# Squared-sum chain of the norm-carrying FFNs, and the block order of the first recurrent mixer

## The reference

```python
def swiglu(h, w1, w3, w2):
    return (jax.nn.silu(h @ w1) * (h @ w3)) @ w2

def half_ffn(x, g, w1, w3, w2):
    return x + FFN_RES * swiglu(rmsnorm(x, g), w1, w3, w2)

def mixer_gla_rglru(h, w_in, ...):               # second stack, layer 0
    q, k, v, g, lr, xr, xg = jnp.split(h @ w_in, MIX0_SPLITS, axis=-1)
    log_f = log_sigmoid(lr @ gla_gate_up + gla_gate_bias) / GLA_GATE_TEMP
    o = chunk_end_gated_linear_attention(q * GLA_DK ** -0.5, k, v, log_f)
    o = rmsnorm(o, gla_head_norm) * silu(g)
    y = rg_lru(causal_depthwise_conv(xr, conv_w, conv_b), lru_wa, lru_ba, lru_wx, lru_bx, lru_lambda)
    y = y * gelu(xg)
    return concatenate([o, y], axis=-1) @ w_out
```

## Time and profile before

| | |
|---|---|
| median of 3 runs | 2967.72 us (2962.85 to 2968.32) |
| the profiled execution | 2967.48 us, span 2965.7 us |
| mean granted TensorE clock | 0.964 of full |
| PE busy | 2743.1 us, 92% |
| POOL busy | 2202.6 us, 74% |
| ACT, DVE busy | 50%, 48% |

### The profile page before, as it was taken

How to read it: one execution, slowest core, us unless ns; L and a number is a source line. 1 busy time by engine, 2 the same in 40 slices (tenths; PEclk the granted TensorE clock), 3 DMA queues, 4 the chain that set the end, 5 groups by cost and what they waited for, 6 DMA issues and landing times.

```text
span 2965.7 us, 59967 instructions
## 1 busy us (share of the span) xinstructions
PE 2743.1 (92%) x21822; PEld 2640.5 (89%) x21822; DVE 1422.3 (48%) x2533; ACT 1483.4 (50%) x2242; POOL 2202.6 (74%) x1680
## 2 busy tenths in 40 slices
PE   8999999979999989999979989997799899998997
PEld 8989898868999989898868989987799799887997
DVE  2134525546556555435546554347533733645335
ACT  4444456445555554456435554455444544555445
POOL 8866666746978967575747968976799689766995
PEclk9999999999999999899989999999899999999999
DMA  6544433424554544343424544543455355433552
GB/s 240 184 149 161 135 131 126 163 86 135 184 170 157 184 156 150 118 151 121 164 93 135 184 149 157 184 149 114 143 185 184 124 180 184 151 130 131 186 184 86
DMA packets 123000, 452.12 MB, mean 152 GB/s; under 512 B 13650, under 2 KB 13650, under 8 KB 122196
## 3 DMA queue, kind: packets, MB, share of 16 engines
q1 hardware_dynamic: 121104, 441.43, 44.4%
q10 hardware_dynamic: 1732, 8.39, 0.8%
HBM read 448.72 MB, written 1.05 MB: 152 GB/s over the span
## 4 chain that ended last, share of the span: by engine, by line
POOL 52%; issue 29%; PE 15%; DVE 2%; ACT 1%; POOLq 1%; DVEq 0%; ACTq 0%
POOL wl L366 27%; POOL wl L367 25%; PE R L405 3%; PE R L401 3%; PE R L404 3%; PE Y L401 1%; PE Y L405 1%; PE Y L404 1%; PE R L549 1%; POOLq L372 0%; PE R L431 0%; PE R L434 0%; PE R L437 0%; DVE W L1920 0%; DVE XLB L1791 0%
## 5 line engine op out<-in xcount | busy, mean ns | idle before, releaser
L366 POOL TENSOR_TENSOR wl<-raw,wh 128x512 fp32r<-128x512 f32 x836 | 1107.8, 1325 | 743.2 <-ACT wh L1074 736.0
L401 PE MATMUL R<-XHB,wh 128*128 128x256 f32 (+1 forms) x4216 | 1205.7, 286 | 25.2 <-POOL wl L367 10.6
L405 PE MATMUL R<-XHB,wl 128*128 128x256 f32 (+1 forms) x4216 | 1198.1, 284 | 0.0
L404 PE MATMUL R<-XLB,wh 128*128 128x256 f32 (+1 forms) x4216 | 1193.9, 283 | 0.0
L367 POOL TENSOR_TENSOR wl<-raw,wh 128x512 fp32r<-128x512 f32 x836 | 1144.5, 1369 | 0.0
L1074 ACT ACTIVATE wh<-raw 128x1024 fp32r<-128x1024 f32 x836 | 878.4, 1058 | 348.2 <-PE R L401 237.0
L401 PEld LDWEIGHTS R<-XHB,wh 128*128 128x128 f32 x4216 | 804.2, 191 | 34.6 <-POOL wl L367 18.2
L404 PEld LDWEIGHTS R<-XLB,wh 128*128 128x128 f32 x4216 | 807.3, 191 | 1.4 <-issue 1.0
L405 PEld LDWEIGHTS R<-XHB,wl 128*128 128x128 f32 x4216 | 805.4, 191 | 0.0
L401 PE MATMUL Y<-BH,wh 128*128 128x256 f32 x1408 | 402.6, 286 | 20.9 <-DVE BL L1722 20.9
L404 PE MATMUL Y<-BL,wh 128*128 128x256 f32 x1408 | 401.1, 285 | 0.0
(11 more groups left out here) (400 smaller groups left out, 3260.0 us busy)
## 6 DMA issues: line engine op xcount, KB each, us to landing
raw<-in_stream SPq DMA_DIRECT2D x836, 512.0 KB, 3.3
G<-in_wcmp ACTq DMA_DIRECT2D x2, 2048.0 KB, 7.8
G<-in_mem ACTq DMA_DIRECT2D x2, 1024.0 KB, 5.9
TB<-in_table SPq DMA_DIRECT2D x1, 1312.0 KB, 13.1
X<-in_x SPq DMA_DIRECT2D x2, 512.0 KB, 5.8
out_dram<-X ACTq DMA_DIRECT2D x4, 256.0 KB, 2.2
WS<-in_mix_w ACTq DMA_DIRECT2D x2, 256.0 KB
G<-in_p ACTq DMA_DIRECT2D x2, 256.0 KB, 3.0
```

Source lines behind the costliest of these rows:

```text
L366: pool.tensor_tensor(wl[:, s, 0:512], raw[:, r, 0:512], wh[:, s, 0:512].bitcast(F32), ALU.subtract)
L401: i = pe.matmul(o, wh[w], hi, start=start, stop=False, skip_group_check=True)
L404: pe.matmul(o, wh[w], lo, start=False, stop=False, skip_group_check=True)
L405: i = pe.matmul(o, wl[w], hi, start=False, stop=stop, skip_group_check=True)
```

## The change

Three things are done.

1. In the seven FFNs DVE adds squares as the pieces are made: after the rests of piece 4, 6 and 7 it adds one pair of square chunks (512 columns) to W8[0:2]. The three adds of `late_root` go. PE sums the two chunks that are left with two matmuls right after `together`, into SQ, the upper half of the fourth Y bank. Three Y banks are zeroed only after the fourth block, ahead of the wait for the first hidden chunk, and the fourth behind that wait. No bank of R is held for the sum. In the ln kind the bank of the mean is handed back as soon as the last chunk is centred. S4 is made while ACT works on the first hidden chunk.
2. `gla` runs in another block order: xr, lr, k0, gate, k1, xg0 to xg3, LRU tiles, v, q0, key-values, q1, g0, state reads, g1, g2, sums, g3. The rows of the output projection are ordered LRU first, then heads.
3. In `gla` work moves from DVE to ACT: the first tap of the convolution, the gate's bias, the square inside gelu, the arguments and the square of the LRU's decay. DVE makes the LRU pieces first, and normalises each pair of heads apart.

PE, and ACT's part:

```diff
+        SQ = Y[:, 3, T:2 * T]
...
 
                 hi, lo, width = (XHB, XLB, T + 2) if kind == "ln" else (XH, XL, T)
-                for b in range(4):
-
+                def opened(b):
                     pe.matmul(Y[:, b, :], ZB[:, 0:P], ZB[:, :], start=True, stop=False, skip_group_check=True)
+
+                if kind == "first":
+                    for b in range(4):
+                        opened(b)
+                if kind == "ln":
+                    means(mean)
...
                     dense(hi, lo, width=width)
                     dense(hi, lo, width=width)
 
-                def down(f, end=None):
+                def down(f, end=None, opens=False):
+                    if opens:
+                        for b in range(3):
+                            opened(b)
                     from_dve()
+                    if opens:
+                        opened(3)
                     s = weights()
                     for c in range(DC):
                         three(Y[:, c // 2, (c % 2) * T:(c % 2) * T + T], (slice(None), s, slice(c * P, c * P + P)),
...
                 together(2, hi, lo, split_ready, width)
                 trips = (FC - 2) // 4
                 if kind != "first":
                     trips -= 1
+                    need(sq_added, 3)
+                    for c in range(2):
+                        i = pe.matmul(SQ, ONES, W8[:, c, :], start=c == 0, stop=c == 1, skip_group_check=True)
+                    i.then_inc(sum_ready, 1)
                     for j in range(4):
-                        dense(hi, lo, width=width)
-                        if j == 0:
-                            need(sq_summed)
-                            pe.matmul(sums[:, T:2 * T], ONES, W8[:, 0, :], start=True, stop=True,
-                                      skip_group_check=True).then_inc(chunk_ready, 1)
-                        dense(hi, lo, width=width)
-                        down(j)
+                        up_pair()
+                        down(j, opens=j == 0)
...
                 i.then_inc(aside_ready, 1)
-                dense(XH, XL)
+                for _ in range(5):
+                    dense(XH, XL)
+                need(lconv_split)
+                s = weights()
+                for j in range(8):
+                    three(claim()[:, 0:T], (slice(None), s, slice(j * P, j * P + P)), BH[:, j % 4, :], BL[:, j % 4, :], True, True,
+                          begins=j == 0, end=chunk_ready)
...
-                s = weights()
-                for j in range(8):
-                    three(claim()[:, 0:T], (slice(None), s, slice(j * P, j * P + P)), BH[:, j % 4, :], BL[:, j % 4, :], True, True,
-                          begins=j == 0, end=chunk_ready)
                 dense(XH, XL)
-                evicted(8)
+                evicted(20)
...
-                m = t.n["chunk"]
-                act.wait_ge(chunk_ready, m + 4)
-                skip(1)
-                step(act.activation(S2[:, 0:T], R[:, m % RING, T:2 * T], ACT.Ln, scale=1.0 / D, bias=EPS[:, eps:eps + 1]))
+                need(sum_ready)
+                step(act.activation(S2[:, 0:T], SQ, ACT.Ln, scale=1.0 / D, bias=EPS[:, eps:eps + 1]))
                 give_dve(act.activation(S3[:, 0:T], S2[:, 0:T], ACT.Exp, scale=-0.5))
...
+                def twice(z, second, func, **how):
+                    split_next()
+                    m, o = chunk()
+                    act.activation(Z[:, z, :], o[:, 0:T], ACT.Copy)
+                    take(act.activation(second, o[:, 0:T], func, **how), m, wait=False)
+
                 for j in range(4):
-                    column(c["xr"] + j)
+                    twice(c["xr"] + j, Z[:, 22 + j, :], ACT.Identity, scale=col("lconv", 12 + j), bias=col("lconv_b", j))
...
-                need(lconv_done)
-                act.activation(BH[:, 0:4, :], Z[:, 22:26, :], ACT.Copy).then_inc(lconv_hi, 1)
+                split_next()
+                o = ready_of("gla", "gate")
+                act.activation(Z[:, 18, :], o[:, 0:T], ACT.Identity, bias=col("gate_b", 0))
+                took_of(act.activation(Z[:, 19, :], o[:, T:2 * T], ACT.Identity, bias=col("gate_b", 1)), "gla", "gate")
+                plain(Z[:, c["k"] + 1, :])
                 act.preload_act_table_set("natural_log_exp_and_others")
-                column(c["k"] + 1)
+                for j in range(2):
+                    twice(c["xg"] + j, G[:, 1, 4 + j, :], ACT.Square)
...
+                need(lconv_done)
+                act.activation(BH[:, 0:4, :], Z[:, 22:26, :], ACT.Copy).then_inc(lconv_hi, 1)
...
+                for j in range(2, 4):
+                    twice(c["xg"] + j, G[:, 1, 4 + j, :], ACT.Square)
+                act.preload_act_table_set("exp_and_others")
                 split_next()
+                for j in range(8):
+                    m, o = chunk()
+                    take(act.activation(W8[:, j, :], o[:, 0:T], ACT.Tanh, scale=0.5, bias=LC[:, 1 + j // 4, j % 4:j % 4 + 1]), m,
+                         wait=j == 7)
...
                 split_next()
+                need(lam_ready)
+                w, a, g = W8[:, 0:4, :], G[:, 0, 4:8, :], G[:, 1, 4:8, :]
+                for j in range(4):
+                    i = act.activation(a[:, j, :], w[:, j, :], ACT.Exp, scale=LC[:, 0, j:j + 1], bias=LC[:, 0, j:j + 1])
+                step(i)
+                for j in range(4):
+                    act.activation(w[:, j, :], w[:, j, :], ACT.Tanh, scale=LC[:, 3, j:j + 1], bias=LC[:, 3, j:j + 1])
+                act.activation(G[:, 0, 0:4, :], a, ACT.Square).then_inc(lru_a, 1)
+                split_next()
+                need(gelu_arg)
+                act.activation(g, g, ACT.Tanh, scale=0.7978845608028654 * 0.044715).then_inc(gelu_tanh, 1)
                 split_next()
...
-                act.preload_act_table_set("exp_and_others")
+                act.preload_act_table_set("natural_log_exp_and_others")
+                column(c["q"], 0.125)
+                need(lru_var)
+                step(act.activation(w, w, ACT.Ln, bias=EPS[:, 3:4]))
+                act.activation(w, w, ACT.Exp, scale=0.5).then_inc(lru_sqrt, 1)
+                column(c["q"] + 1, 0.125)
...
-                column(c["xg"] + 3)
+                split_next()
+                split_next()
...
-
-                def gate(j):
-                    split_next()
+                split_next()
+                for j in range(4):
                     m, o = chunk()
                     act.activation(M[:, 4 + j, :], o[:, 0:T], ACT.Tanh, scale=0.5).then_inc(tanh_done, 1)
...
+                piece_hi(0, flat(Z[:, 18:20, :]))
+                piece_hi(1, flat(Z[:, 20:22, :]))
                 split_next()
-                piece_hi(1, flat(Z[:, 18:20, :]))
-                piece_hi(2, flat(Z[:, 20:22, :]))
+                piece_hi(2, flat(O[:, 0:2, :]))
                 piece_hi(3, flat(O[:, 2:4, :]))
```

DVE in the FFNs:

```diff
-            def hidden_rms(j):
+            def hidden_rms(j, opens=False):
                 e, h, a, v = EB[:, j % 2, :], HID[:, j % 2, :], M[:, 2 + j % 2, :], HID[:, 2 + j % 2, :]
                 m, o = chunk()
                 give_act(tt_(a, o[:, 0:T], S3[:, 0:T], ALU.mult))
+                if opens:
+                    step(stt(S4[:, 0:T], S3[:, 0:T], 0.25, S3[:, 0:T], ALU.mult, ALU.mult))
...
                 give_pe(stt(XL[:, c, :], X[:, c, :], gain(c), XH[:, c, :].bitcast(F32), ALU.mult, ALU.subtract))
+                if c in (4, 6, 7):
+                    need(x_squared, 2 if c == 4 else 1)
+                    w = flat(W8[:, 0:2, :])
+                    give(tt_(w, w, flat(W8[:, 2 * (c // 2) - 2 if c < 7 else 6:2 * (c // 2) if c < 7 else 8, :]), ALU.add), sq_added)
 
             def late_root(eps):
 
-                need(x_squared, 4)
-                step(tt_(flat(W8[:, 0:4, :]), flat(W8[:, 0:4, :]), flat(W8[:, 4:8, :]), ALU.add))
-                step(tt_(flat(W8[:, 0:2, :]), flat(W8[:, 0:2, :]), flat(W8[:, 2:4, :]), ALU.add))
-                give(tt_(W8[:, 0, :], W8[:, 0, :], W8[:, 1, :], ALU.add), sq_summed)
                 from_act()
-                m = t.n["chunk"]
-                skip(1)
-                v, y, w, q = S2[:, 0:T], S3[:, 0:T], S4[:, T:2 * T], S4[:, 0:T]
-                take(ts_(v, R[:, m % RING, T:2 * T], 1.0 / D, eps, ALU.mult, ALU.add), m)
+                v, y, w = S2[:, 0:T], S3[:, 0:T], S4[:, T:2 * T]
+                step(ts_(v, SQ, 1.0 / D, eps, ALU.mult, ALU.add))
                 step(tt_(w, y, y, ALU.mult))
                 step(stt(w, w, -0.5, v, ALU.mult, ALU.mult))
                 step(stt(y, w, 1.5, y, ALU.add, ALU.mult))
-                if eps == RMS_EPS:
```

DVE in the mixer:

```diff
-                    step(ts_(y, x, col("lconv", 12 + j), col("lconv_b", j), ALU.mult, ALU.add))
...
-                o, x, e = ready("gate"), Z[:, 18:20, :], Z[:, 20:22, :]
-                step(ts_(x[:, 0, :], o[:, 0:T], col("gate_b", 0), None, ALU.add))
-                took(ts_(x[:, 1, :], o[:, T:2 * T], col("gate_b", 1), None, ALU.add), "gate")
```

(40 more changed lines are left out.)

94 lines of the change are left out of this document (34 added, 60 removed).

## The result

The changed kernel takes 2946.63 us (median of 4 runs, 2942.66 to 2950.04) against 2967.55 us for the kernel before in the same comparison. The ratio is 0.9944, 95% interval 0.9932 to 0.9955: 21 us faster by the medians, 16.6 us by the ratio. The forecast was 38 us. The profiled execution took 2942.66 us with a span of 2940.9 us, at a mean granted clock of 0.970 of full (0.964 before).

The account below looks back on a forecast made before the run. The prediction took PE to set the pace, with time to gain only in its pauses and low-clock stretches. Heads 15.2, clock 8 and mixer 15 us summed to 38.2 off, giving 2929.5 us; forecast 2923 to 2936, 8-in-10 range 2914 to 2948.

Parts of the forecast that it names:

- The step that failed: FFN heads, Ln to first down product: 8.30 us before, less S4, plus a zeroing; net 2.0 us gained per ln head.
- Ln 1.95 us sooner (ln), 2.25 (rms): FFN heads: Ln starts earlier because the sum of squares is ready sooner, by 1.95 us (ln) or 2.25 (rms).
- `together` 1.3 us longer in the ln heads: Ln FFN heads: two adds between the pieces make the last piece and the end of `together` 1.3 us later.
- The bank's wait of 1.63 is no gain of its own: FFN heads: the 1.63 us wait goes, filled from the last wait, which stays at 1.6 (ln) or 0.4 (rms).
- Zeroing costs nothing: FFN heads: zeroing three banks is hidden in PE's last wait; without that wait it would cost 0.7 us a head.
- The clock, 8 us: Behind the FFN heads: most low-clock stretches go as waits shrink, 8 us gained, bounds 0 and 11.4.
- The mixer, 15 us: Recurrent mixer: old pauses of 26.3 us give way to new ones of 11.7; 15 us gained, bounds 8 and 20.
- (b): FFN heads: gain taken back, adds meet POOL and low clock stays; 2941.5 us, up to 2949 with weaker mixer; 14%.
- (a): Mixer: its last part stays bound by DVE, so only 6 of the 15 us come; 2938.5 us; 17%.
- (c): Heads and mixer: all low-clock stretches go and the mixer gives 20 us; 2921 us, 2914 at the end; 10%.
- (d): FFN bodies: POOL becomes the bound and the kernel is slower, 2998 us at 3.0 us a block; 4%.
- (e): Mixer: the moved LRU block makes PE wait as long as before, and the heads give 4 us; 2963 us; 4%.

Follow-up runs that it names:

- experiment 3: The changed kernel with the FFN root's intermediate value kept in the sum's half bank of PSUM: 2925.16 us, ratio 0.987 to the kernel before.
- experiment 4: The kernel before with ACT's third rounding moved ahead of Ln, so POOL works during the old root: 2974.38 us, ratio 1.0036.
- experiment 6: The changed kernel with three of the four Y banks zeroed again at the start of the head: 2945.86 us, ratio 0.9935 to the kernel before.
- experiment 5: The changed kernel with the three zeroings ahead of the first down product repeated to keep PE busy: 2937.48 us, ratio 0.9909 to the kernel before.
- experiment 2: The kernel before with only the mixer part of the change, FFN heads untouched: 2946.97 us, ratio 0.9943.
- experiment 8: The changed kernel with the root's value in PSUM in the FFNs and the first recurrent mixer's head norms: 2924.28 us, ratio 0.987 to the kernel before.
- experiment 1: The kernel before with only the FFN head part of the change, old mixer: 2968.8 us against 2964.41, ratio 1.0012.

## Why the prediction was wrong

**The step that failed** is in the part on the heads: "From Ln to the first down product it took 8.30 us. S4 leaves this chain ... Net 2.0 us a head". I carried the old duration of a chain on DVE to another moment. The root's instructions had been short because POOL was idle just then, and moving Ln 1.9 us forward put them on POOL's rests of the fourth block and of the one for the first down product. The duration read from the row was right for its moment and wrong for the new one. Measured, the chain takes 9.89 us (8.0 expected) in the ln head and 8.82 (6.8) in the first rms head. That is the balance of two things: in the ln head the root's three instructions take 2.7 us more, and the product behind the Tanh, which now misses POOL, 0.84 less. I did weigh the contention, but only for the adds, where it was not what decided: in the first ln head the three took 0.69 each, as I had taken them. The Trainium skill (SBUF — State Buffer, "Who interferes with whom") says that a DVE instruction with at most one SBUF input, outside the two-port modes, does not contend with GpSimd. Experiments 3 and 4 agree: 0.43 with one of the two inputs in PSUM, and 1.38 to 1.41 with both in SBUF beside a working POOL. The same section counts a `tensor_scalar` in a two-port mode among those that contend; S4 of the ln heads, a `tensor_scalar` of 0.29 us alone and of 1.48 beside POOL in experiment 3, fits that, though no run here shows which mode it is in.

**Ln 1.95 us sooner (ln), 2.25 (rms).** The first is right: 1.92. The second was 3 us too large over four heads: 1.54, 0.85, 2.64 and 0.97, 6.0 in place of 9.0. It took the pace of `together` from the kernel before; the first 5.70 us of it in the four heads hold 135 matmuls in place of 161, which is 3.1 us. The prediction counted the low clock only behind the heads, and moving the zeroings leaves the pauses ahead of `together` unbroken. That this is the cause is argued and not shown (experiment 6).

**`together` 1.3 us longer in the ln heads.** Right: from its first matmul to its end it takes 8.71 us in place of 7.31, 1.40 more, with PE's wait of 0.72 and shorter ones inside.

**The bank's wait of 1.63 is no gain of its own.** Right: it is gone from all seven heads, the 0.64 from the ln heads, and the last wait took their place. It ended near 3.5 (ln) and mostly at 2.5 to 2.9 (rms) rather than at 1.6 and 0.4. With the PSUM root the rms value was 0.38, so 0.4 was the right number for the case in which nothing meets POOL.

**Zeroing costs nothing.** Right for the time as a whole, by experiment 6.

**The clock, 8 us.** This fell with the step above, since the waits did not shrink: 85 matmuls missing in place of 100, 1.8 us. That the stretches hang on the waits was right. Filler in the waits brought them all back (experiment 5), and shorter waits brought back 57 matmuls, 6.8 us (experiment 3).

**The mixer, 15 us.** Right in size, a little low: 17 us by experiment 2. The wait in the LRU block was 2.06 (2.9 expected), ahead of the output 5.44 (4.4), inside it 1.78 (4.0); 1.11 (0.69 before) and 0.76 came that I had not listed. First matmul to first output chunk took 93.6 us (97). Here too DVE's two-input instructions met POOL, for 2.4 us by experiment 8.

**The rivals.** (b) is what happened, for a reason that it did not hold: "the adds meet POOL" was its cause, the root meeting POOL was the real one, and that its price of 2941.5 to 2949 contains the 2946.6 is partly luck: it had the heads lose 12 of their 23 us and a weaker mixer, where the heads lost all 23 (experiment 1) and the mixer gave 2 more than forecast. (a) is false, the mixer gave all of its 15. (c) did not come with this change: the clock stayed low behind six of the seven heads. (d) did not happen: POOL ends no wait in the bodies. (e) did not happen: the mixer's gain is there.

**The sum again.** 38 forecast. With the root's instructions given one PSUM operand the same change gives 39 us (ratio 0.987), so one meeting of two engines was worth 22 us by the ratios. That 39 lies so near to 38 is in part luck: in experiment 3 the ln waits are still 2.3, 2.2 and 1.5 us where 1.6 was forecast and the rms heads' Ln still comes late in two heads, while the mixer gives more than its 15.
